# Differential attention heads: the two probability maps subtracted ahead of the transposes, in a two-layer flow-matching step

## What is computed

```python
def _diff_out(o1, o2, lam_l, lam_init, subln_l):
    ...
    o = o1 - lam.astype(o1.dtype) * o2
    return _rmsnorm(o, subln_l) * (1.0 - lam_init)

ob = _diff_out(_sdpa(q1, k1, v_all), _sdpa(q2, k2, v_all), lam_l, lam_init, subln_l)
```

## Time and profile before

| | |
|---|---|
| median of 3 runs | 1704.3 us (1703.79 to 1707.12) |
| profiled execution, its own time | 1709.76 us |
| its span, first to last instruction | 1708.0 us |
| TensorE / weight load / VectorE / ScalarE busy | 94% / 78% / 70% / 56% |
| mean granted TensorE clock | 0.955 of full |
| attention items of layer 0 / layer 1 | about 112 to 182 us / 529 to 598 us |

### The profile page before, as it was taken

One profiled execution on the slowest core, in us unless ns is written; L12 is line 12 of the kernel. 1 busy time (PEld: TensorE's weight loads), 2 busy tenths in 40 slices (PEclk: granted clock), 3 DMA queues, 4 the chain that ended last, 5 costly groups with the idle time before them and its releaser, 6 DMA issues.

```text
span 1708.0 us, 23134 instructions
## 1 busy us (share of the span) xinstructions
PE 1609.8 (94%) x8263; PEld 1327.0 (78%) x8263; DVE 1203.2 (70%) x1041; ACT 964.6 (56%) x917; POOL 90.0 (5%) x142
## 2 busy tenths in 40 slices
PE   5989879999898887999999999999999999999996
PEld 3857769998686767888888888888888888888884
DVE  2456444443636643888988988988988888888885
ACT  3333334333533341777677777677677776776773
POOL 2420040000011010000000000000000000000001
PEclk7998899999998985999999999999999999999998
DMA  9854374566752443898998998998998998998991
GB/s 371 260 186 151 122 212 162 197 200 239 258 192 92 143 139 115 297 367 317 365 371 319 360 372 316 362 371 318 363 368 318 366 366 316 369 364 324 362 365 42
DMA packets 218290, 473.85 MB, mean 277 GB/s; under 512 B 8464, under 2 KB 41536, under 8 KB 218240
## 3 DMA queue, kind: packets, MB, share of 16 engines
q1 hardware_dynamic: 215024, 466.38, 76.6%
q0 software_dynamic: 3216, 6.79, 1.4%
HBM read 470.62 MB, written 2.52 MB: 277 GB/s over the span
## 4 chain that ended last, share of the span: by engine, by line
PE 90%; DVE 5%; ACT 2%; issue 1%; DMA 1%; POOL 1%; SPq 0%; POOLq 0%; DVEq 0%; ACTq 0%
PE ps L1528 22%; PE ps L1529 22%; PE ps L1533 22%; PE ps L1543 3%; PE ps L1550 3%; PE ps L1544 3%; PE ps L1913 2%; PE ps L1742 2%; PE ps L1573 2%; PE ps L1706 2%; PE ps L1925 1%; PE ps L1585 1%; PE ps L1616 1%; DMA raw<-in_w_ada 1%; DVE region L1092 1%
## 5 line engine op out<-in xcount | busy, mean ns | idle before, releaser
L1044 DVE TENSOR_TENSOR w_lo<-raw,w_hi 128x2048 fp32r<-128x2048 f32 (+1 forms) x397 | 903.5, 2285 | 189.9 <-ACT w_hi L716 189.4
L716 ACT ACTIVATE w_hi<-raw 128x2048 fp32r<-128x2048 f32 (+1 forms) x397 | 758.1, 1914 | 256.9 <-PE ps L1529 236.7
L1528 PE MATMUL ps<-w_hi,x_hi 128*128 128x512 f32 (+1 forms) x1216 | 439.1, 372 | 9.0 <-issue 6.3
L1529 PE MATMUL ps<-w_hi,x_lo 128*128 128x512 f32 (+1 forms) x1216 | 430.3, 365 | 0.0
L1533 PE MATMUL ps<-w_lo,x_hi 128*128 128x512 f32 (+1 forms) x1216 | 285.1, 364 | 0.0
L1528 PEld LDWEIGHTS ps<-w_hi,x_hi 128*128 128x128 f32 x1216 | 230.8, 190 | 49.6 <-issue 11.8
L1529 PEld LDWEIGHTS ps<-w_hi,x_lo 128*128 128x128 f32 x1216 | 230.7, 190 | 36.1
L1533 PEld LDWEIGHTS ps<-w_lo,x_hi 128*128 128x128 f32 x1216 | 207.3, 188 | 39.6
L1528 PE MATMUL ps<-w_hi,h_hi 128*128 128x512 f32 x528 | 208.2, 394 | 0.0
L1529 PE MATMUL ps<-w_hi,h_lo 128*128 128x512 f32 x528 | 207.8, 394 | 0.0
L1533 PE MATMUL ps<-w_lo,h_hi 128*128 128x512 f32 x528 | 141.6, 393 | 0.0
(11 more groups left out here) (241 smaller groups left out, 1263.9 us busy)
## 6 DMA issues: line engine op xcount, KB each, us to landing
raw<-in_moe_w_gate SPq DMA_DIRECT2D x112, 1024.0 KB, 5.2
raw<-in_moe_w_up SPq DMA_DIRECT2D x112, 1024.0 KB, 5.3
raw<-in_moe_w_down SPq DMA_DIRECT2D x112, 1024.0 KB, 5.3
raw<-in_w_ada SPq DMA_DIRECT2D x48, 1024.0 KB, 6.1
raw<-in_w_in SPq DMA_DIRECT2D x20, 960.0 KB, 9.9
raw<-in_ffn_w_gate SPq DMA_DIRECT2D x11, 1024.0 KB, 5.5
raw<-in_ffn_w_up SPq DMA_DIRECT2D x11, 1024.0 KB, 7.2
raw<-in_ffn_w_down SPq DMA_DIRECT2D x11, 1024.0 KB, 5.1
```

Of the source, the lines that this page charges most:

```text
L716: act.activation(split_hi(c, slice(0, width(c))), raw[:, r % NRAW, 0:width(c)], ACT.Copy).then_inc(hi_done, 1)
L1044: dve.tensor_sub(split_lo(c, n), raw[:, raw_of(c) % NRAW, n], split_hi(c, n)).then_inc(lo_done, 1)
L1528: pe.matmul(out, xh, split_hi(c, w), start=start, stop=False, skip_group_check=True)
L1529: last = pe.matmul(out, xl, split_hi(c, w), start=False, stop=False, skip_group_check=True)
```

## The change

VectorE subtracts the two maps of a head in `probs` before TensorE turns them. A new function `soft_diff` waits for the exponentials of item i, takes the reciprocals, makes the factor -lambda * sum1 / sum2 for each of two heads, and writes P1 + factor * P2 over P1, one instruction of 128 (s = 0) or 256 (s = 1) columns a head. A new semaphore, `diff_ready`, releases the turning. `item_T` then turns two blocks (s = 0) or four (s = 1) instead of four or eight, and `item_out` multiplies two maps instead of four. The copies out of PSUM are 256 wide instead of 512, the scaling of the output is over 128 columns and is by the first map's reciprocal, and the combination behind it is gone. Other items keep their steps.

```diff
--- before.py
+++ after.py
@@ -327,7 +327,7 @@
         qr_ready = sem("qr_ready")
         prep_mm = [sem("prep_mm0"), sem("prep_mm1")]
         prep_evac = [sem("prep_evac0"), sem("prep_evac1")]
-        scores, sm_bias, probs_ready, pT, pt_evac, o_mm, o_evac = (sem(n) for n in ("scores", "softmax_bias", "probs_ready", "probs_T", "probs_T_evac", "o_mm", "o_evac"))
+        scores, sm_bias, probs_ready, diff_ready, pT, pt_evac, o_mm, o_evac = (sem(n) for n in ("scores", "softmax_bias", "probs_ready", "maps_subtracted", "probs_T", "probs_T_evac", "o_mm", "o_evac"))
         sink_d, sink_e = sem("sink_arg"), sem("sink_exp")
         lam_s, lam_e = sem("lam_sums"), sem("lam_exp")
         dsq, drs, o_ready, oT, o_hi, o_lo = (sem(n) for n in ("diff_sq", "diff_rstd", "o_ready", "o_T", "o_hi", "o_lo"))
@@ -1174,13 +1174,30 @@
                 dve.tensor_scalar(nb, sm[:, s, 24:28], -1.0, None, ALU.mult).then_inc(sm_bias, 1)
                 dve.tensor_sub(sm[:, s, 12:16], sink, sm[:, s, 24:28]).then_inc(sink_d, 1)
 
+            def soft_diff(l, i):
+
+                s = i % 2
+                nk = nk_of(s)
+                dve.wait_ge(probs_ready, 10 * l + i + 1)
+                link(dve.reciprocal(sm[:, s, 20:24], sm[:, s, 8:12]))
+                link(dve.scalar_tensor_tensor(out=sm[:, s, 24:26], in0=sm[:, s, 8:12:2], scalar=lam[:, 4:5], in1=sm[:, s, 21:24:2],
+                                              op0=ALU.mult, op1=ALU.mult))
+                for h in range(2):
+                    last = dve.scalar_tensor_tensor(out=probs[:, s, 2 * h, 0:nk], in0=probs[:, s, 2 * h + 1, 0:nk],
+                                                    scalar=sm[:, s, 24 + h:25 + h], in1=probs[:, s, 2 * h, 0:nk],
+                                                    op0=ALU.mult, op1=ALU.add)
+                last.then_inc(diff_ready, 1)
+
             def soft_T(l, i):
 
                 s = i % 2
+                n = 2 * P if ITEMS[i // 2] in ("B0", "B1") else 4 * P
                 dve.wait_ge(pT, 10 * l + i + 1)
                 for kb in range(1 + s):
-                    last = dve.tensor_copy(pt_sb[kb], ps[:, kb, :])
+                    last = dve.tensor_copy(pt_sb[kb][:, 0:n], ps[:, kb, 0:n])
                 last.then_inc(pt_evac, 1)
+                if ITEMS[i // 2] in ("B0", "B1"):
+                    return
                 if ITEMS[i // 2] == "A":
                     dve.wait_ge(sink_e, 2 * l + s + 1)
                     link(dve.tensor_add(sm[:, s, 8:12], sm[:, s, 8:12], sm[:, s, 16:20]))
@@ -1190,18 +1207,15 @@
                 it, s = ITEMS[i // 2], i % 2
                 n = 10 * l + i + 1
                 dve.wait_ge(o_mm, n)
-                o = out_view(s).rearrange("p (h d) -> p h d", h=4)
-                r = b2(sm[:, s, 20:24], HD)
                 if it not in ("B0", "B1"):
-                    dve.tensor_tensor(xn[:, s, O_COL[it]:O_COL[it] + 256].rearrange("p (h d) -> p h d", h=4), o, r,
-                                      ALU.mult).then_inc(o_evac, 1)
+                    o = out_view(s).rearrange("p (h d) -> p h d", h=4)
+                    dve.tensor_tensor(xn[:, s, O_COL[it]:O_COL[it] + 256].rearrange("p (h d) -> p h d", h=4), o,
+                                      b2(sm[:, s, 20:24], HD), ALU.mult).then_inc(o_evac, 1)
                     return
-                t = otmp[:, :].rearrange("p (h m d) -> p h m d", h=2, m=2)
-                dve.tensor_tensor(otmp[:, :].rearrange("p (h d) -> p h d", h=4), o, r, ALU.mult).then_inc(o_evac, 1)
+                o = out_view(s)[:, 0:P].rearrange("p (h d) -> p h d", h=2)
+                ob = xn[:, s, O_COL[it]:O_COL[it] + P].rearrange("p (h d) -> p h d", h=2)
+                dve.tensor_tensor(ob, o, b2(sm[:, s, 20:24:2], HD), ALU.mult).then_inc(o_evac, 1)
                 dve.wait_ge(o_evac, n)
-                ob = xn[:, s, O_COL[it]:O_COL[it] + P].rearrange("p (h d) -> p h d", h=2)
-                link(dve.scalar_tensor_tensor(out=ob, in0=t[:, :, 1, :], scalar=lam[:, 4:5], in1=t[:, :, 0, :],
-                                              op0=ALU.mult, op1=ALU.add))
                 if it == "B1":
                     o4 = xn[:, s, 256:512]
                     link(dve.tensor_mul(otmp[:, :], o4, o4))
@@ -1463,6 +1477,8 @@
                 for i in range(10):
                     if i + 1 < 10:
                         soft_pre(l, i + 1)
+                    if ITEMS[i // 2] in ("B0", "B1"):
+                        soft_diff(l, i)
                     soft_T(l, i)
                     if i in (1, 3, 5, 7):
                         prep(l, len(FIRST[1]) + i // 2)
@@ -1711,14 +1727,18 @@
 
             def item_T(l, i):
                 n = 10 * l + i
-                pe.wait_ge(probs_ready, n + 1)
+                pairs = ITEMS[i // 2] in ("B0", "B1")
+                if pairs:
+                    pe.wait_ge(diff_ready, 4 * l + i - 1)
+                else:
+                    pe.wait_ge(probs_ready, n + 1)
                 if n:
                     pe.wait_ge(pt_evac, n)
                 if i in (3, 5, 9):
                     pe.wait_ge(mod_ready, SECTIONS.index((l, {3: 2, 5: 3, 9: 4}[i])) + 1)
                 for kb in range(1 + i % 2):
-                    for h in range(4):
-                        last = pe.transpose(ps[:, kb, cols(h, P)], probs[:, i % 2, h, cols(kb, P)], ident())
+                    for h in range(2 if pairs else 4):
+                        last = pe.transpose(ps[:, kb, cols(h, P)], probs[:, i % 2, 2 * h if pairs else h, cols(kb, P)], ident())
                 last.then_inc(pT, 1)
 
             def item_out(l, i):
@@ -1727,7 +1747,7 @@
                 pe.wait_ge(pt_evac, n + 1)
                 if n:
                     pe.wait_ge(o_evac, n)
-                for h in range(4):
+                for h in range(2 if it in ("B0", "B1") else 4):
                     if it == "A":
                         vs = (proj[s][:, VA + HD * (h // 2):VA + HD * (h // 2) + HD],
                               vcache[:, V_W + HD * (h // 2):V_W + HD * (h // 2) + HD])
@@ -1736,7 +1756,7 @@
                     elif it == "C":
                         vs = [v_mla[s][:, cols(4 * kb + h, HD)] for kb in range(1 + s)]
                     else:
-                        g = 2 * int(it[1]) + h // 2
+                        g = 2 * int(it[1]) + h
                         vs = (proj[s][:, VB + HD * g:VB + HD * g + HD], vcache[:, V_D + HD * g:V_D + HD * g + HD])
                     for kb in range(1 + s):
                         last = pe.matmul(out_view(s)[:, cols(h, HD)], pt_sb[kb][:, cols(h, P)], vs[kb],
```

## The result

The changed kernel took **1727.4 us** (median of 4 runs, 1723.3 to 1730.3) against 1704.1 us, a ratio of 1.0129 with a 95% interval from 1.0114 to 1.0143. That is 23.3 us slower, in the direction that was forecast, at twice its size and above its range. The profiled execution took 1727.91 us; its span is 1726.1 us against 1708.0 us, 18.1 us more. The profile of before was itself 5.7 us over its median, which is why the spans differ by less than the medians do.

A forecast was written before the change was run, and what follows sets the result against it. TensorE alone was taken to bound the B items; 9.8 us added less 5.0 saved a layer makes 9.6 us in both, plus 2 for the clock: +11.6 us on the median 1704.3, so 1716 us, range 1708 to 1722.

The forecast's parts named there:

- What the change takes: In the B items, halved turning (2.1 us) and halved value matmuls (2.9 us) take 5.0 us a layer off TensorE.
- first rival: Clock holds at 1.00 in the B items, both slow stretches go: net +2.4 us a layer, 1709 us; chance 0.10.
- What it adds, and where: TensorE idles ahead of each B item's turning for VectorE's reduction and subtraction, 2.57 or 2.33 us: +9.8 us a layer.
- What it calls nothing: Later DMA fetches in the B items, begun 2.5 us later, still land in time: priced at nothing.
- the clock: TensorE's granted clock in the B items: one more slow stretch a layer, 1.0 us each, +2 us in all.
- second rival: Every new idle stretch in the B items brings a slow one, two to four more a layer: 1720 to 1727 us; chance 0.15.
- fourth rival: No wait ahead of the turning, subtraction done before the next scores end; only 5.0 us a layer saved: 1694 us; chance 0.02.

The follow-up runs named there:

- e3: The changed kernel without the subtraction and TensorE's wait for it, turning and value matmuls in the B items still halved; 1690.3 us, ratio 0.9927.
- e2: The changed kernel with two extra 128x512 matmuls of constants on TensorE ahead of each B item's turning; 1712.6 us, ratio 1.0055.
- e6: The changed kernel with eight extra 128x2 matmuls on TensorE ahead of each B item's turning; 1730.5 us, ratio 1.017.
- e7: The changed kernel with sixteen extra 128x128 transposes of a constant on TensorE ahead of each B item's turning; 1712.4 us, ratio 1.0053.
- e8: The changed kernel with VectorE's subtraction moved earlier, ahead of the modulation section, and ScalarE's exponentials of item 4 ahead of the modulation row copy; 1695.0 us, ratio 0.9944.
- e1: The changed kernel with VectorE's subtraction for item i moved ahead of the reduction for item i+1; 1705.6 us, ratio 1.001.
- e4: The kernel before with the subtraction and TensorE's wait for it added, all four maps still turned and multiplied; 1736.3 us, ratio 1.0198.

## Why the prediction was wrong

Right, by its own steps:

- *What the change takes.* 10 us of TensorE's work were forecast; e3 gave 14 us, the surplus with less slow time. Its layer 1, at full clock, is 7.3 us shorter than before, where 5.0 and the first rival's 2.4 make 7.4.
- *What it adds, and where.* TensorE does wait ahead of every turning, for the reasons given. It idled 9.7 and 9.6 us in the two stretches (35.19 - 25.46, 41.29 - 31.70) where 9.8 was forecast, and the pairs of subtractions took 0.62 and 0.89 us on the chain where 0.61 and 0.87 were. The estimate of 474 ns for 256 columns measured 481.
- *What it calls nothing.* No fetch came late; DMA queues appear nowhere in the chain of the stretches.

**The step that failed is the clock**: "I expect one slow stretch more in a layer. It would cost ... 1.0 us, +2 us in all". The mechanism was named, but the term was mis-sized by a factor of five to six. Both its count and its price were low. In the profiled pair the slow time rose by 27.5 us (13.2 to 40.7 us), which is eight stretches of 3.4 us rather than two.

What they cost: of the 23.3 us, 9.6 are the waits less the savings as forecast and 1.8 the turnings behind the waits, which leaves 11.9 us; in the profiled pair 21.5 - 11.4 = 10.1 us, 1.3 for each of the eight, not 1.0. In layer 0 both slow stretches of after begin in a wait (PEclk 0.59 over 136.10 to 138.39, with TensorE idle, and 0.60 over 152.87 to 156.27); in layer 1 both begin within 1 us behind one (1.00 over 555.38 to 556.27, then 0.52 over the 1.78 us behind it; 0.88 over 576.12 to 577.03, then 0.50). From there they go on over the preparation, the modulation matmuls and the columns.

e2 and e6 show that what counts is that hardly anything streams in the waits: wide fillers took away nearly all slow time and 14.8 us, which is the price of the added slow time and of that of before together, and narrow ones took away nothing of the 1727.4 us. The weighing of the two pulls was the error: fewer short matmuls against new idle time were taken as nearly even, though the first removes 2.9 us a layer of 64-column matmuls and the second adds 9.8 us in which nothing streams.

**A smaller term was left out.** The prediction halved the turning, 0.44 to 0.22 us for an even item. That holds where nothing waits (e3); behind a wait the two blocks took 0.44 and four took 0.66, which is 0.22 us a wait and 1.8 us in all, priced at nothing. What sets that extra time was not looked into; the weight load of the first block starts only when the wait ends (130.88).

The second rival ("every new idle stretch brings a slow one", 1720 to 1727 us) comes closest to what happened, at a chance of 0.15, and the range ended inside it. It allowed two to four slow stretches more in a layer and there were two in layer 0 and six in layer 1; the measured 1727.4 us is its upper end. The argument held against it, that half clock keeps the engine occupied twice as long and so works against a second fall, did not hold: layer 1 was slow for 27.3 of 41.3 us. That layer 0 and layer 1 differ by 6.1 us with the same instructions stays open in part: the slow times say by what (13.4 and 27.3 us), but what decides where a fall comes was not tested.

The first rival's price (1709 us, clock held at 1.00) is 3.5 us under what e2 and e7 reached by force. The fourth rival's (no wait, 1694) is near e8, where nearly all of the wait is taken away, but partly by luck: it counted no gain of the clock, and with no wait at all e3 took 1690.3.

## What to carry to other kernels

When an engine that works through a fixed order gets a new operand from another engine, look at what that other engine must do first: of each wait of 2.3 to 2.6 us here, the subtraction was 1.0 to 1.3 and its place behind another reduction in VectorE's order the rest. Moving it to where VectorE already waited, and ScalarE's exponentials ahead of a copy that waited, turned +23 us into -10. Moving it by one place only (e1) gave back 22 us and left other work of VectorE ahead of it. Price idle time on TensorE at more than its length: in this kernel 20 us of waits cost 32. If a wait can't be removed, filling it with wide matmuls or transposes is worth a try; narrow ones gained nothing here.

## What the runs showed of the hardware

- The clock was at half for 20.2 us of a stretch in which TensorE was busy 96% (37.19 of 38.91 us, PEclk 0.74) when its waits held matmuls of 2 columns, and stayed at 1.00 and 0.95 when the same waits held matmuls of 512 columns. A busy share alone doesn't tell whether the clock will hold.
- Transposes kept it up as well as matmuls did: 1712.4 against 1712.6 us. The Trainium skill, "TensorE: Matmul & The Clock Gate", Part 4 on the PE-mode transpose, says that transposes don't count as TensorE activity for the clock in the way that matmuls do. The traces of this case, with fp32 blocks of 128x128, do not agree: PEclk 0.95 and 0.95 with the transposes, 0.81 and 0.67 with the waits left empty.
- The Trainium skill, "TensorE: Matmul & The Clock Gate", section "HAM oscillation — how this bites in real kernels", blames waits between bursts of matmuls, of some 3 to 5 us in its example. In e4, with TensorE's instructions unchanged, waits of 2.3 to 3.0 us took the slow time from 6.6 and 6.6 to 10.2 and 13.7 us, so the trace agrees, and with shorter waits than in that example. The section does not cover the falls of before, which came with TensorE busy throughout.
- Behind a wait of 2.3 to 2.6 us the first turning took 0.22 us more than without one (0.44 against 0.22 for two blocks, 0.66 against 0.44 for four, all at full clock).
- A slow clock moved by some us changes parts of the kernel that nobody touched: two groups of gate matmuls (16 records each) took 3.80 and 3.77 us before and 2.06 and 2.04 after.
